# Queries and keys of the second and third mixers: products of 512 and 256 columns in two PSUM banks, cross sums added by VectorE

## The reference

```
fox:  q, k, v, fz = split(h_norm @ w_in);  s = q @ k.T / 8 + cum_q - cum_k;  p = softmax(s);  o = p @ v;  h += o @ w_out
dil:  u, q, k, v  = split(n @ w_in);       s = q @ k.T / 8 - slope * dist;   softmax over three dilations;   h += gate * (concat(pool(u), o) @ w_out)
```

## Time and profile before

| | |
|---|---|
| median of 3 runs | 1081.07 us (1080.84 to 1081.16) |
| the profiled execution: its own time, its span | 1081.0 us, 1079.2 us |
| granted TensorE clock, mean | 0.998 of full speed |
| fox: first unit of queries and keys starts, `out_fox` starts | 344.24 us, 401.99 us |
| dil: the same | 824.09 us, 854.64 us |

### The profile page before, as it was taken

One profiled execution on the slowest core, in us unless ns is written; L12 is line 12 of the kernel. 1 busy time (PEld: TensorE's weight loads), 2 busy tenths in 40 slices (PEclk: granted clock), 3 DMA queues, 4 the chain that ended last, 5 costly groups with the idle time before them and its releaser, 6 DMA issues.

```text
span 1079.2 us, 16107 instructions
## 1 busy us (share of the span) xinstructions
PE 1067.3 (99%) x6102; PEld 916.8 (85%) x6102; DVE 792.6 (73%) x1388; ACT 669.3 (62%) x1182; POOL 121.8 (11%) x212
## 2 busy tenths in 40 slices
PE   9999999999999999999999999999999999999997
PEld 8998788888888998888888788888878978888885
DVE  7767678787876776777677787988785777566575
ACT  7678677565666776766565765454476767445443
POOL 1133110110100531020000000111010210000000
PEclk9999999999999999999999999999999999999999
DMA  9932259788865643687777468878755445555551
GB/s 360 329 121 92 105 185 337 283 311 292 314 208 176 217 139 105 228 309 276 269 257 269 157 213 295 297 255 333 265 173 178 138 147 185 196 195 192 184 189 61
DMA packets 65534, 238.33 MB, mean 221 GB/s; under 512 B 7430, under 2 KB 8614, under 8 KB 64689
## 3 DMA queue, kind: packets, MB, share of 16 engines
q1 hardware_dynamic: 51696, 188.82, 51.2%
q0 software_dynamic: 13040, 47.85, 12.0%
q10 hardware_dynamic: 720, 0.62, 0.2%
HBM read 236.15 MB, written 1.11 MB: 220 GB/s over the span
## 4 chain that ended last, share of the span: by engine, by line
PE 90%; DVE 6%; ACT 2%; issue 1%; DMA 0%; POOL 0%; DVEq 0%; ACTq 0%
PE bank L1694 23%; PE bank L1663 15%; PE bank L1664 15%; PE bank L1665 15%; PE bank L1698 12%; PE bank L1818 2%; DVE w_lo L1136 2%; PE bank L1882 1%; PE bank L1864 1%; PE bank L1856 1%; PE bank L1855 1%; DVE tok L1156 1%; PE bank L1715 1%; PE bank L1764 1%; PE bank L1719 1%
## 5 line engine op out<-in xcount | busy, mean ns | idle before, releaser
L1136 DVE TENSOR_TENSOR w_lo<-raw,w_hi 128x1024 fp32r<-128x1024 f32 x348 | 413.7, 1227 | 69.2 <-ACT w_hi L729 66.7
L729 ACT ACTIVATE w_hi<-raw 128x1024 fp32r<-128x1024 f32 x345 | 348.8, 1052 | 65.1 <-DMA raw<-in_stream 64.6
L1694 PE MATMUL bank<-a_two,w_hi 128*128 128x512 f32 x1088 | 271.9, 392 | 0.0
L1694 PEld LDWEIGHTS bank<-a_two,w_hi 128*128 128x128 f32 x1088 | 198.4, 188 | 37.4
L1663 PE MATMUL bank<-w_lo,hid_hi 128*128 128x512 f32 x432 | 169.1, 391 | 0.2
L941 ACT ACTIVATE cross<-bank 128x256 f32<-128x256 f32 x136 | 51.5, 381 | 189.2 <-PE bank L1698 189.0
L1664 PE MATMUL bank<-w_hi,hid_lo 128*128 128x512 f32 x432 | 168.7, 390 | 0.0
L1665 PE MATMUL bank<-w_hi,hid_hi 128*128 128x512 f32 x432 | 168.1, 389 | 0.0
L1698 PEld LDWEIGHTS bank<-a_two,w_lo 128*128 128x128 f32 x1088 | 148.4, 190 | 10.6
L1698 PE MATMUL bank<-a_two,w_lo 128*128 128x256 f32 x1088 | 151.7, 282 | 0.0
L1385 DVE TENSOR_TENSOR hid_act<-bank,cross 128x256 f32<-128x256 f32 x96 | 39.5, 421 | 86.5 <-ACT cross L941 86.4
(11 more groups left out here) (235 smaller groups left out, 1356.1 us busy)
## 6 DMA issues: line engine op xcount, KB each, us to landing
raw<-in_stream SPq DMA_DIRECT2D x348, 512.0 KB, 5.0
ada_raw<-in_ada POOLq DMA_DIRECT2D x72, 512.0 KB, 5.4
cmpw<-in_stream SPq DMA_DIRECT2D x4, 1024.0 KB, 9.3
rel_band<-rel_scratch POOLq DMA_DIRECT2D x2, 1024.0 KB, 9.3
cum_row<-cum_scratch POOLq DMA_DIRECT2D x4, 512.0 KB, 4.8
gate_row<-gate_scratch POOLq DMA_DIRECT2D x3, 512.0 KB, 6.1
h<-in_x SPq DMA_DIRECT2D x2, 512.0 KB, 4.6
silu_row<-in_c_row POOLq DMA_DIRECT2D x2, 512.0 KB, 6.3
```

The costliest lines, as they stand in the source:

```text
L729: nc.scalar.activation(w_hi[:, u % RING, part_], raw[:, u % RING, part_], ACT.Copy).then_inc(hi_ready, 1)
L1136: nc.vector.tensor_tensor(w_lo[:, u % RING, part_], raw[:, u % RING, part_], w_hi[:, u % RING, part_].bitcast(F32), ALU.subtract).then_inc ...
L1694: nc.tensor.matmul(ps[bank][:, 0:2 * T], wh[:, k, cols_], a_two[:, :, k, :], start=k == 0, stop=False)
```

## The change

The queries and keys of the fox and dil mixers go over to the form of the MLPs. A new function `wide_feature` computes one group of 128 features in each tick: 8 matmuls of 512 columns and 8 of 256, into one bank. The unit now takes a pair of banks, (4, 7) or (2, 5) by turns. All eight banks become one PSUM tensor, and the numbers are assigned so that the banks of a pair lie side by side and one instruction can read both. ScalarE copies the first halves of the two banks as before. VectorE has two operations for each half of the partitions where it had one: first bank times gain less the rounded value into a scratch tile `split`, then, after a wait for that, the second half of the banks times gain plus `split`. In the fox mixer the first unit waits for the forget gates to have left bank 7; in the dil mixer the pooling moves from the banks 7 and 2 to the banks 0 and 3.

```diff
-        ps = [ctx.enter_context(nc.psum_tensor(f"bank{i}", [P, 512], F32)) for i in range(8)]
+        banks = ctx.enter_context(nc.psum_tensor("bank", [P, 8, 512], F32))
+        ps = [banks[:, i, :] for i in (0, 1, 2, 7, 4, 3, 6, 5)]
+        split = place("split", [P, 2, T], at=V_at + 4 * D * 4)
+        def two_banks(rows_, pair_, part):
+            return banks[rows_, pair_[0]:pair_[0] + 2, part * T:(part + 1) * T]
...
+        WIDE = ("qk_fox", "qk_dil")
-            STACKS[("qk_fox", j_)] = (4 + j_ % 2, j_ % 2 == 0, 2 * (j_ // 2))
+            STACKS[("qk_fox", j_)] = (((4, 7), (2, 5))[j_ % 2], j_ % 2 == 0, 2 * (j_ // 2))
...
                 # ScalarE, stack
-                    src = ps[bank][HD * b:HD * b + HD, :].rearrange("p (a b) -> p a b", a=2)
+                    rows_ = slice(HD * b, HD * b + HD)
+                    if key[0] in WIDE:
+                        src = two_banks(rows_, bank, 0)
...
                 # VectorE, stack
+                    if key[0] in WIDE:
+                        gain = 1.0 if keys else -0.125
+                        chain(nc.vector.scalar_tensor_tensor(out=split[rows_, :, :], in0=two_banks(rows_, bank, 0), scalar=gain,
+                                                             in1=hi.bitcast(F32), op0=ALU.mult, op1=ALU.subtract))
+                        nc.vector.scalar_tensor_tensor(out=dst, in0=two_banks(rows_, bank, 1), scalar=gain, in1=split[rows_, :, :],
+                                                       op0=ALU.mult, op1=ALU.add).then_inc(feat_taken, 1)
+                        continue
...
                 # TensorE
+            def wide_feature(u, bank, nt):
+                wh = w_hi[:, u % RING, :].rearrange("p (k c) -> p k c", k=KT)
+                wl = w_lo[:, u % RING, :].rearrange("p (k c) -> p k c", k=KT)
+                cols_ = slice(nt * P, nt * P + P)
+                for half in range(2):
+                    pe.wait_ge(hi_ready, 2 * u + half + 1)
+                    for k in range(4 * half, 4 * half + 4):
+                        nc.tensor.matmul(ps[bank][:, 0:2 * T], wh[:, k, cols_], a_two[:, :, k, :], start=k == 0, stop=False)
+                for half in range(2):
+                    wait_weights(u, half)
+                    for k in range(4 * half, 4 * half + 4):
+                        ins = nc.tensor.matmul(ps[bank][:, T:2 * T], wl[:, k, cols_], a_hi[:, k, :], start=False, stop=k == KT - 1)
+                return ins
...
+                if tick.tag in WIDE:
+                    if (tick.tag, tick.j, tick.part) == ("qk_fox", 0, 0):
+                        pe.wait_ge(fz_taken, 1)
+                    ins = wide_feature(tick.u, STACKS[(tick.tag, tick.j)][0][tick.part], tick.part)
+                    if tick.part == 1:
+                        ins.then_inc(unit_used, 1)
+                    return
...
-                                ins = nc.tensor.matmul(ps[(7, 2)[c]][:, (g % 2) * T:(g % 2 + 1) * T], u_rows[:, k, g * P:(g + 1) * P],
+                                ins = nc.tensor.matmul(ps[(0, 3)[c]][:, (g % 2) * T:(g % 2 + 1) * T], u_rows[:, k, g * P:(g + 1) * P],
```

More of the change, by code:

```diff
@@ L468, in build @@
                   ("qm0", 0): (4, False, 0), ("km0", 0): (5, True, 0), ("km1", 0): (4, True, 2), ("qm1", 0): (5, False, 2)}
+        WIDE = ("qk_fox", "qk_dil")
         for j_ in range(8):
-            STACKS[("qk_fox", j_)] = (4 + j_ % 2, j_ % 2 == 0, 2 * (j_ // 2))
+            STACKS[("qk_fox", j_)] = (((4, 7), (2, 5))[j_ % 2], j_ % 2 == 0, 2 * (j_ // 2))
         for j_ in range(4):
-            STACKS[("qk_dil", j_)] = (4 + j_ % 2, j_ % 2 == 0, 2 * (j_ // 2))
+            STACKS[("qk_dil", j_)] = (((4, 7), (2, 5))[j_ % 2], j_ % 2 == 0, 2 * (j_ // 2))
         STACK_NO = {key: n_ for n_, key in enumerate(STACKS)}
@@ L860, in stack @@
                 for b in range(2):
-                    src = ps[bank][HD * b:HD * b + HD, :].rearrange("p (a b) -> p a b", a=2)
+                    rows_ = slice(HD * b, HD * b + HD)
+                    if key[0] in WIDE:
+                        src = two_banks(rows_, bank, 0)
+                    else:
+                        src = ps[bank][rows_, :].rearrange("p (a b) -> p a b", a=2)
                     for half in ((b, 1 - b) if keys else (b,)):
@@ L1090, in dil_extras @@
                         act.wait_ge(pooled_done, c + 1)
-                        nc.scalar.activation(pooledT[:, 2 * c:2 * c + 2, :], ps[(7, 2)[c]][:, :].rearrange("p (g t) -> p g t", g=2),
+                        nc.scalar.activation(pooledT[:, 2 * c:2 * c + 2, :], ps[(0, 3)[c]][:, :].rearrange("p (g t) -> p g t", g=2),
                                              ACT.Copy).then_inc(pooled_taken, 1)
@@ L1098, in dil_extras @@
                             m = 2 * c + k
-                            ins = nc.scalar.activation(q_two[:, 4 + m, 0, :], ps[(7, 2)[c]][:, k * T:(k + 1) * T],
+                            ins = nc.scalar.activation(q_two[:, 4 + m, 0, :], ps[(0, 3)[c]][:, k * T:(k + 1) * T],
                                                        ACT.Identity, scale=pc_("pool_scale", 1, m))
@@ L1329, in stack @@
                     rows_ = slice(HD * b, HD * b + HD)
-                    src = ps[bank][rows_, :].rearrange("p (a b) -> p a b", a=2)
                     hi = (k_two if keys else q_two)[rows_, tile:tile + 2, b, :]
                     dst = k_lo2[rows_, tile:tile + 2, b, :] if keys else q_two[HD * (1 - b):HD * (1 - b) + HD, tile:tile + 2, b, :]
+                    if key[0] in WIDE:
[5 more added lines that the diff above has]
+                        continue
+                    src = ps[bank][rows_, :].rearrange("p (a b) -> p a b", a=2)
                     ins = nc.vector.scalar_tensor_tensor(out=dst, in0=src, scalar=1.0 if keys else -0.125, in1=hi.bitcast(F32),
@@ L1626, in dil_extras @@
                             ins = nc.vector.scalar_tensor_tensor(
-                                out=q_two[:, 4 + m, 1, :], in0=ps[(7, 2)[c]][:, k * T:(k + 1) * T], scalar=pc_("pool_scale", 1, m),
+                                out=q_two[:, 4 + m, 1, :], in0=ps[(0, 3)[c]][:, k * T:(k + 1) * T], scalar=pc_("pool_scale", 1, m),
                                 in1=q_two[:, 4 + m, 0, :].bitcast(F32), op0=ALU.mult, op1=ALU.subtract)
@@ L2140, in dil_extras @@
                         for g in (2 * c, 2 * c + 1):
-                            ins = nc.tensor.matmul(ps[(7, 2)[c]][:, (g % 2) * T:(g % 2 + 1) * T], w_pool[:, g, :], pooledT[:, g, :],
+                            ins = nc.tensor.matmul(ps[(0, 3)[c]][:, (g % 2) * T:(g % 2 + 1) * T], w_pool[:, g, :], pooledT[:, g, :],
                                                    start=True, stop=True)
```

## The result

The changed kernel takes 1083.81 us (median of 9 runs, 1083.74 to 1083.97), the kernel before 1081.07 (9 runs): +2.74 us, a ratio of 1.0026 with a 95% interval of 1.0016 to 1.0036. The profiled execution has 1083.8 us, a span of 1082.0 and a mean clock of 0.998. The forecast was 1083.5.

A forecast was written before the change was run, and what follows sets the result against it. TensorE, busy 99% of the span, was taken as the bound. Terms -2.4 (matmuls) + 2.9 (two ends) + 1.3 (fox's queue) + 0.7 (dil's queue) = +2.5 us gave 1083.5 us, range 1080.9 to 1085.4.

The forecast's parts named there:

- Matmuls: Fox's and dil's twelve units of queries and keys: 16 fewer matmuls gain 0.20 us a unit, -2.4 us in all.
- rival D: The wide form gains only what the page's rule gives, 0.5 us in place of 2.4: 1085.4 us; chance 0.03.
- The two ends: Starts of `out_fox` and `out_dil`: added operations in the last stack delay TensorE by 1.44 us each, +2.9 us together.
- VectorE's queue: While heads run, VectorE falls behind and stalls TensorE: +1.3 us in fox, +0.7 us in dil.
- A lateness of 1.13 us on top: Fox, transposes after the copy of probabilities at 370.95: lateness exceeds the remaining 0.76 us of slack, stall some 0.4 us.
- two periods that were named as short: Fox, between row minima: 369.56 to 376.83 is 0.28 us too little, the one ending at 393.01 is 1.13.
- 1.64 needed: VectorE between two heads' row minima: 1.44 us of added operations plus TensorE's unit 0.20 us shorter.
- Costed at nothing: Bank 7's wait, pooling in banks 0 and 3, weights, ScalarE's rounding, loads and moved banks: no cost.
- wait for bank 7: Fox's first unit: VectorE reads the bank last at 336.84, 7.4 us before that unit, so no cost.
- A: Only the ends of the mixers cost, -2.4 + 2.9 = +0.5: 1081.5 us; chance 0.25.
- B: Last stack of each mixer: added operations run inside VectorE's wait for ScalarE's copies, whole gain kept, 1078.6 us; chance 0.05.
- C: VectorE becomes the bound, passing lateness to and from ScalarE from unit to unit: 1085.3 us; chance 0.17.

The follow-up runs named there:

- e1: Changed kernel with one VectorE operation for each half of the rows again, TensorE's wide form kept: 1078.89 us against 1080.96 before.
- e3: Changed kernel with the last unit of each mixer narrow, one operation for each half of the rows: 1081.26 us against 1080.96 before.
- e5: Changed kernel with VectorE's reciprocal moved ahead of the half of the weights' rest part in queries' and keys' ticks: 1083.53 us against 1080.88 before.
- e9: Changed kernel with GpSimd scaling a head's 128 columns first and its 256 columns second: 1083.03 us against 1080.91 before.
- e10: Changed kernel with no wide unit, only the new order of banks and the moved pooling: 1080.86 us against 1080.91 before.
- e11: Changed kernel with one more chained VectorE operation for each half of the rows: 1101.68 us against 1080.91 before.
- e4: Changed kernel with the wide form and two operations only in the first two units of each mixer: 1080.77 us against 1080.96 before.
- e8: Changed kernel, wide only in units 0, 1, 4 and 6 of fox and 0 and 1 of dil: 1080.25 us against 1080.88 before.
- e12: Changed kernel, wide only in fox units 0, 1, 4, 6 and dil 0, 1, with GpSimd's smaller scaling first: 1079.74 us against 1080.82 before.

## Why the prediction was right

Forecast 1083.5 us, measured 1083.81; the direction, the size and the largest term hold. One term, the queue's, came near in size although its chain was wrong, and that is luck. Point by point:

- **Matmuls, -2.4 us.** Measured -2.1 (e1, 1.1 to 3.1 by its interval), and 0.18 us a unit in place of 0.20 (13.95 against 14.39 us for two and a half units), 2.2 for twelve. The mechanism is right, the size 0.2 to 0.3 too large: the earlier trace rows is one unit between its neighbours, a longer stretch would have given the pitch better. The 0.5 us of rival D lie outside the interval.
- **The two ends, +2.9 us.** e3 gives 2.9 by the times and 2.65 by the rows. The chain was read rightly from the earlier trace rows, and the added operations take 0.68 to 0.69 us with 0.03 to 0.04 between, so 0.72 each and no penalty for two banks.
- **VectorE's queue, +1.3 and +0.7 us.** From the rest, 2.74 + 2.1 - 2.9 = 1.9 us against 2.0. By the stages, and with the forecast's 1.44 for each end, fox lost 1.53 + 8 x 0.18 - 1.44 = 1.5 us and dil 1.27 + 4 x 0.18 - 1.44 = 0.55. The total is right, the way was for the most part not. The step "A lateness of 1.13 us on top uses up the other 0.76 and stalls TensorE by some 0.4 us at this place" looked for the stall at the copy of the probabilities; there it is 0.24 us, between heads 10 and 11. The largest stall, 0.83 us, came by a chain that the prediction doesn't have: stack, weights, reciprocal, GpSimd, transposes. Removing it gives 0.6 us in fox (e5, e9), though in e5 the loss at the row minimum grows by 0.18. I had costed GpSimd at nothing, and had not seen that its pair is held off by VectorE's subtraction of weights, though rows of the kernel before show such pairs at 1.88 us. Of the two periods that were named as short, the one of 1.13 us has the 0.24 behind it, and the one that starts at 369.56, short by 0.28, cost at most 0.04. The 0.83 and the 0.21 us before it belong to the stack of the period ahead of it, which the prediction left out. In the kernel before, VectorE's spare time there is in these brackets and the 0.61 us before the row minimum at 369.56:

```profile
363.40 0.68 DVE L1333 SCALAR_TENSOR_TENSOR k_lo<-bank,k_two 64x512 fp32r<-64x512 f32 x1 [0.17 <-ACT k_two L863]
364.62 0.69 DVE L1333 SCALAR_TENSOR_TENSOR k_lo<-bank,k_two 64x512 fp32r<-64x512 f32 x1 [0.54 <-ACT k_two L863]
365.57 1.23 DVE L1136 TENSOR_TENSOR w_lo<-raw,w_hi 128x1024 fp32r<-128x1024 f32 x1 [0.25 <-ACT w_hi L729]
```

  That is 1.57 us against the 1.64 needed: by the prediction's own count almost enough. A sum over a whole period doesn't see a reciprocal in the middle of it that comes 0.65 us later (366.72 before, 367.37 after).
- **Costed at nothing.** Banks, pooling and the wait for bank 7: e10, 1080.86 against 1080.91 us.
- **The rivals.** A (only the ends) is refuted by the 1.4 us lost inside fox's units and by e9. B (won back inside a wait for ScalarE) by e3, and by the timeline at the ends, where VectorE has no pause. C (VectorE is the bound) did not happen: TensorE's waits don't go on in every unit. With one more operation it is there (e11). D by e1.

## What to carry to other kernels

An operation added to an engine with time to spare cost nothing here as long as no other engine waited for what stood behind it in the list (e4). So look at the spare time between two waits of that stretch, not at the share of the stage: here VectorE had 28% free, and 17 us of added work cost 4.9, while the next 17 cost 17.9. The last item before a change of stage has no cover, so keep its form short even if the others get the longer one (e3), and use the new form only where the list has room (e8, e12). And follow the chain to its last link: here TensorE waited behind a late reciprocal of 0.16 us.

## What the runs showed of the hardware that was not expected

GpSimd's scaling of 128 x 256 and 128 x 128 elements takes 0.82 us alone and 1.88 us when VectorE's 1.22 us subtraction of two SBUF operands begins beside its second half; with the smaller operation first it is 0.83 us, and the subtraction takes 1.40 (e9). One VectorE operation that reads 64 x 2 x 256 elements from two PSUM banks takes what it takes from one, 0.69 us. And after waits of 0.91 and 1.57 us close together TensorE's granted clock stood at 0.50 for the next two microseconds (e11), where waits of 0.42 and 0.84 us left it at 1.00.
